# Attention scores in two passes over 128 stacked rows instead of three over 64

## The chip, the cores and the metric
One NeuronCore of a Trainium2 chip runs the whole program. The metric is device time in microseconds, the median over runs of one launch. The profile is one execution recorded by the hardware profiler.

## What is computed
A two-layer decoder trunk on 1024 tokens of width 1024, in float32. Layer 0 is a gated short convolution with a SwiGLU feed-forward block. Layer 1 is attention with 16 heads of width 64 over keys and values made once from the residual stream, again followed by a feed-forward block. Only the attention matters here:

```python
q = (x @ w_q).reshape(b, s, N_HEADS, HEAD_DIM) * (HEAD_DIM ** -0.5)
...
sc = jnp.einsum("bnqrhe,bnkrhe->bnrhqk", qb, k_cat).astype(jnp.float32)
...
sc = jnp.where(valid[:, None, None], sc + bias, -jnp.inf)
m = jnp.max(sc, axis=-1, keepdims=True)
p = jnp.exp(sc - m)
...
wts = jax.nn.softmax(jnp.stack(lses), axis=0)
o = jnp.sum(wts[..., None] * jnp.stack(outs), axis=0)
```

The three dilated branches are merged by their softmax denominators. The kernel computes this as one causal attention per head whose bias holds the ALiBi slope and the logarithm of how many branches see a key.

## The kernel before, in words
Float32 products are made from parts that TensorE takes in one pass (type fp32r): every operand is split into a high part and a low part, and a product is high·high + high·low + low·high, three passes that add up in PSUM. ScalarE makes high parts (a copy with a cast), VectorE low parts (a subtraction).

The program is written engine by engine. Each engine has its own list of instructions in a fixed order, and semaphores named after what is done (`q_lo_done`, `s_done`, `max_done`) tie them together. There is no scheduler: what stands in an engine's list behind a waiting instruction waits too. All weight loads stand in one list on SP (the SyncE queue).

The attention stage goes by pairs of heads, since two heads of 64 fill 128 partitions. There are 8 pairs. Six run in a loop of three turns with two pairs each, the last two are written out. A pair has 16 steps (`STEPS`): step `s` treats head `s // 8` of the pair and query block `s % 8` of 128 tokens, against the `s % 8 + 1` key blocks that it may see. A step with few blocks is short, one with eight is long. In step `s` TensorE does, in this order (`attend` in its block):

- `scores(s + 1)`: the scores of the next step, up to 1024 columns in the two SCORE banks, after VectorE has taken the maximum of the scores before (`max_done`),
- a third of the step's share of projection matmuls for the next pair,
- `turn_part(s - 2)`: one transpose of an output sum (`o_sum`),
- `turn_probs(s)`: the transposes of the exponentials, one per key block,
- a second third of the projection matmuls,
- `outputs(s - 1)`: probabilities times values, one matmul per key block,
- the last third.

Meanwhile VectorE adds the bias and takes the maximum (L1338), makes the low part of the transposed probabilities (L1354) and the output sum (L1370); ScalarE does the exponentials (L1005), the high part of the probabilities (L949), half of the output (L957) and the division (L965).

The projections of the next pair (keys, values, queries, each in two halves of 512 tokens, 24 matmuls per half) fill TensorE's time in between. They are cut into runs of three matmuls: 48 runs, and `slots` says how many runs each of the 16 steps gets. `END_RUNS` of the last step's runs are kept for the end of the pair, between the last outputs. `ends_in[j]` is the step in which half `j` ends (0, 1 keys, 2, 3 values, 4, 5 queries), and one step later ScalarE and VectorE turn it into high and low parts, behind their other work of that step. With `slots` all 3 this is step 14 for the first half of the queries. Its high and low parts are what the first score of the next pair, issued as `scores(16)` in step 15, needs:

```python
halves = moving * 2 + (2 * pair + 1 + i // 4)
pe.wait_ge(*q_lo_done.at("attn", halves))
...
passes = (("q_hi", "k_hi"), ("q_hi", "k_lo"), ("q_lo", "k_hi"))
```

A head's queries and keys lie in 64 of the 128 partitions (`rows`), so each score matmul contracts over 64 rows. Query parts have one buffer, key parts two (one per pair in turn).

Of the kernel before, what the change touches and what calls it, by code (L numbers as in the profile page):

```python
# [21 lines left out]
F32 = mybir.dt.float32  # L22
F32R = mybir.dt.float32r
# [3 lines left out]
ALU = mybir.AluOpType  # L27
ACT = mybir.ActivationFunctionType

P = 128  # L30
# [29 lines left out]
def trunk(nc, x, norm_g, conv_in_w, conv_w, conv_out_w, kv_norm_g, kv_w, q_w, o_w,  # L60
# [23 lines left out]
    with ExitStack() as ctx:  # L84
# [72 lines left out]
        spilled, x_back, stored = sem("spilled"), sem("x_back"), sem("stored")  # L157

# [125 lines left out]
        slots = [3, 3, 3, 3, 3, 3, 3, 3, 3, 3, 3, 3, 3, 3, 3, 3]  # L284
        END_RUNS = 3
# [8 lines left out]
        def _(sp):  # L294
            def column_chunk(w, col):

                return w.rearrange("(k p) n -> p k n", p=P)[:, :, bass.ds(col, P)]
# [12 lines left out]
            def load_two_row_blocks(ph, w):  # L310

                for c in range(KT):
                    half, q = c // (KT // 2), c % (KT // 2)
                    load((chunk0[ph] + c, 0),
                         w.rearrange("(k p) n -> p k n", p=P)[:, 2 * q:2 * q + 2,
                                                             half * HALF:(half + 1) * HALF])
# [50 lines left out]
            load_two_row_blocks("conv_out", conv_out_w[0])  # L367
            load_ffn("ffn0", 0)
            with sp.Fori(0, PAIRS // 2) as g:
                for pos in range(6):  # L370
                    col = g * (2 * P) + (pos // 3) * P
                    src = (kv_w, kv_w, q_w[0])[pos % 3]
                    load((chunk0["attn"] + pos, g * 6),
                         column_chunk(src, col + (D if pos % 3 == 1 else 0)))
            load_two_row_blocks("oproj", o_w[0])
# [8 lines left out]
        def _(pe):  # L384
# [214 lines left out]
            def attend(a, after):  # L599
# [6 lines left out]
                def scores(s):  # L606
                    pair, s_in = fixed + s // STEPS, s % STEPS
                    e, i = s_in // TT, s_in % TT
                    rows = slice(HD * e, HD * e + HD)
# [14 lines left out]
                    mm.then_inc(s_done.sem, 1)  # L624
# [87 lines left out]
            pe.wait_ge(*q_lo_done.at("attn", 1))  # L712
            for n, (q, k) in enumerate((("q_hi", "k_hi"), ("q_hi", "k_lo"), ("q_lo", "k_hi"))):
                mm = pe.matmul(psum[:, SCORE, 0:P], att[q][0:HD, 0:P], att[k][0:HD, 0, 0:P],
                               start=(n == 0), stop=(n == 2))
# [14 lines left out]
        def _(act):  # L730
# [178 lines left out]
            def project(r, j):  # L909

                moving, fixed = r
                part, h = j // 2, j % 2
                cols = slice(h * HALF, (h + 1) * HALF)
                product("attn", h, moving * 3 + (3 * fixed + part + 1),
                        moving * 3 + (3 * fixed + part + 1))
                if part == 0:
                    act.copy(att["k_hi"][:, fixed % 2, cols], bank(PROJ + h)) \
                        .then_inc(k_hi_done.sem, 1)
                elif part == 1:

                    act.wait_ge(*v_turned.at("attn", moving * 2 + (2 * fixed + h)))
                    act.copy(att["v_t"][:], bank(PROJ + h)).then_inc(v_done.sem, 1)
                else:

                    act.wait_ge(*s_done.at("attn", moving * STEPS
                                           + (fixed * STEPS - (1 - h) * TT // 2)))
                    act.activation(att["q_hi"][:, cols], bank(PROJ + h), ACT.Copy,
                                   scale=-float(HD) ** -0.5).then_inc(q_hi_done.sem, 1)
# [107 lines left out]
        def _(dve):  # L1036
# [254 lines left out]
            def project(r, j):  # L1291
# [5 lines left out]
                if part == 0:  # L1297
                    dve.wait_ge(*k_hi_done.at("attn", count))
                    dve.tensor_tensor(att["k_lo"][:, fixed % 2, cols], bank(PROJ + h),
                                      f32(att["k_hi"][:, fixed % 2, cols]), ALU.subtract) \  # L1300
                       .then_inc(k_lo_done.sem, 1)
                elif part == 2:
                    dve.wait_ge(*q_hi_done.at("attn", count))
                    dve.scalar_tensor_tensor(out=att["q_lo"][:, cols], in0=bank(PROJ + h),
                                             scalar=-float(HD) ** -0.5,
                                             in1=f32(att["q_hi"][:, cols]),
# [272 lines left out]
```

## Time and profile before

| | |
|---|---|
| median of 3 runs | 2700.91 us |
| lowest and highest | 2696.95 and 2702.74 us |
| span of the profiled execution | 2691.9 us |
| TensorE busy | 2549.6 us, 95% of the span |
| VectorE, ScalarE, GpSimd busy | 1120.2, 725.3 and 247.6 us |
| attention stage, pairs 1 to 7 and the last | from about 1225 to 1821 us of the span |

The span runs from the first to the last instruction; a run's time is some us longer, and for the profiled execution only the span is recorded. In the profile PE is TensorE, DVE is VectorE, ACT is ScalarE, POOL is GpSimd and SPq is the queue of SyncE. A line such as L620 is a line of the kernel before. Matmuls overlap in the pipeline and their ends are modelled, so what one costs is read from its start to the next start.

### The profile page before, as it was taken

Reading aid. Unit: us, or ns where it says so; the run is one execution under the profiler, and the core shown is the slowest. Engines: PE = TensorE matmul, PEld = TensorE weight load, DVE = VectorE, ACT = ScalarE, POOL = GpSimd, SP = SyncE. Lnnn points to the kernel's source line nnn. Section 1 sums busy time; section 2 is a strip of 40 time slices with the busy share of each in tenths; the row PEclk is TensorE's granted clock in tenths of the full one; section 3 lists DMA queues with packets and bytes.
Section 4 is the critical chain, followed back from the end, with each engine's and each line's share of the span. In section 5 each row is a group of like instructions: output and inputs, shape, how many; then the busy total and the mean of one; then the engine's idle time right before and its main releaser. Section 6 shows DMA issues by size and latency. Waiting matters only on the chain.

```text
span 2691.9 us, 32590 instructions
## 1 busy us (share of the span) xinstructions
PE 2549.6 (95%) x11648; PEld 2059.7 (77%) x11648; DVE 1120.2 (42%) x1686; ACT 725.3 (27%) x1328; POOL 247.6 (9%) x344
## 2 busy tenths in 40 slices
PE   7999989999999999969999999989799999999996
PEld 6888767888888888757777777767688888888885
DVE  4333243333333333574555555552533333333335
ACT  3111142111111111234544455552421111111112
POOL 1000031000000000241111111100500000000004
PEclk9999989999999999989999999989899999999998
DMA  4111111111111111120000000003021111111111
GB/s 126 47 54 47 55 40 48 47 50 51 47 47 47 47 47 48 38 83 28 24 20 20 24 16 24 24 1 118 24 63 47 47 47 47 47 47 47 47 47 70
DMA packets 162799, 124.18 MB, mean 46 GB/s; under 512 B 8736, under 2 KB 148000, under 8 KB 162720
## 3 DMA queue, kind: packets, MB, share of 16 engines
q1 hardware_dynamic: 159776, 111.71, 13.4%
q10 hardware_dynamic: 2944, 11.53, 1.2%
q8 instruction: 36, 0.59, 0.1%
q14 instruction: 43, 0.35, 0.0%
HBM read 114.84 MB, written 8.39 MB: 46 GB/s over the span
## 4 chain that ended last, share of the span: by engine, by line
PE 87%; issue 4%; POOL 3%; DVE 3%; ACT 2%; DMA 0%; SPq 0%; POOLq 0%; DVEq 0%; ACTq 0%
PE banks L397 46%; PE banks L539 17%; PE banks L583 9%; PE banks L474 5%; PE banks L620 5%; PE banks L632 2%; PE banks L645 2%; POOL resid L1483 2%; POOL rstd L1450 1%; PE banks L436 1%; PE banks L659 1%; POOL mean L1444 1%; DVE x_lo L1061 1%; ACT scores L1005 0%; ACT junk L773 0%
## 5 line engine op out<-in xcount | busy, mean ns | idle before, releaser
L1049 DVE TENSOR_TENSOR w_lo<-raw,w_hi 128x1024 fp32r<-128x1024 f32 x196 | 240.5, 1227 | 588.0 <-ACT w_hi L751 586.8
L397 PE MATMUL banks<-x_hi,w_hi 128*128 128x512 f32 x1792 | 449.1, 393 | 20.9 <-DVE x_lo L1061 20.9
L397 PE MATMUL banks<-x_lo,w_hi 128*128 128x512 f32 x1792 | 444.8, 390 | 0.0
L397 PE MATMUL banks<-x_hi,w_lo 128*128 128x512 f32 x1792 | 442.6, 389 | 0.0
L751 ACT CAST w_hi<-raw 128x1024 fp32r<-128x1024 f32 x196 | 205.5, 1049 | 809.6 <-PE banks L539 428.4
L397 PEld LDWEIGHTS banks<-x_hi,w_hi 128*128 128x128 f32 x1792 | 338.9, 190 | 93.8 <-issue 14.9
L397 PEld LDWEIGHTS banks<-x_lo,w_hi 128*128 128x128 f32 x1792 | 336.8, 188 | 69.8
L397 PEld LDWEIGHTS banks<-x_hi,w_lo 128*128 128x128 f32 x1792 | 336.4, 188 | 69.9
L1092 DVE TENSOR_TENSOR acc<-acc,banks 128x512 f32<-128x512 f32 x352 | 240.5, 687 | 209.4 <-PE banks L539 209.4
L539 PE MATMUL banks<-w_hi,hid_hi 128*128 128x512 f32 x704 | 224.4, 400 | 5.8 <-issue 4.7
L539 PE MATMUL banks<-w_lo,hid_hi 128*128 128x512 f32 x704 | 223.6, 399 | 0.0
L539 PE MATMUL banks<-w_hi,hid_lo 128*128 128x512 f32 x704 | 223.1, 398 | 0.0
L1214 DVE TENSOR_TENSOR hid<-silu_gate,banks 128x512 f32<-128x512 f32 x88 | 60.5, 688 | 319.9 <-PE banks L397 319.9
L539 PEld LDWEIGHTS banks<-w_hi,hid_hi 128*128 128x128 f32 x704 | 133.3, 190 | 38.7 <-issue 5.5
L539 PEld LDWEIGHTS banks<-w_lo,hid_hi 128*128 128x128 f32 x704 | 134.0, 190 | 32.5
L539 PEld LDWEIGHTS banks<-w_hi,hid_lo 128*128 128x128 f32 x704 | 133.7, 190 | 32.4
L870 ACT ACTIVATE silu_gate<-banks 128x512 f32<-128x512 f32 x88 | 52.8, 600 | 326.6 <-PE banks L397 326.5
L1354 DVE TENSOR_TENSOR pt<-banks,pt 128x128 fp32r<-128x128 f32 (+7 forms) x128 | 96.9, 757 | 100.3 <-ACT pt L949 100.2
L1338 DVE CUSTOM_DVE_ANT_0 scores<-banks,bias 128x128 f32<-128x128 f32 (+7 forms) x128 | 96.8, 756 | 95.1 <-PE banks L620 86.9
L583 PE MATMUL banks<-x_hi,w_hi 128*128 128x512 f32 x384 | 120.3, 426 | 11.2 <-DVE x_lo L1061 11.2
L583 PE MATMUL banks<-x_lo,w_hi 128*128 128x512 f32 x384 | 127.6, 423 | 0.0
L583 PE MATMUL banks<-x_hi,w_lo 128*128 128x512 f32 x384 | 117.0, 411 | 0.0
(116 smaller groups left out, 2631.1 us busy)
## 6 DMA issues: line engine op xcount, KB each, us to landing
raw<-in_ffn_in_w SPq DMA_DIRECT2D x88, 512.0 KB, 3.7
raw<-in_ffn_out_w SPq DMA_DIRECT2D x44, 512.0 KB, 3.2
raw<-in_conv_in_w SPq DMA_DIRECT2D x24, 512.0 KB, 3.7
raw<-in_kv_w SPq DMA_DIRECT2D x16, 512.0 KB, 3.9
resid<-in_x SPq DMA_DIRECT2D x8, 512.0 KB, 7.1
raw<-in_conv_out_w SPq DMA_DIRECT2D x8, 512.0 KB, 3.2
raw<-in_q_w SPq DMA_DIRECT2D x8, 512.0 KB, 3.8
x_spill<-resid ACTq DMA_DIRECT2D x1, 4096.0 KB, 12.8
```

Source lines behind the costliest of these rows:

```text
L397: mm = pe.matmul(bank(out_bank), w[:, slot, k * P:(k + 1) * P], a[:, k, h * HALF:(h + 1) * HALF], start=(i == 0), stop=(i == len(passes) - 1))
L474: mm = pe.matmul(bank(t), a[:, 2 * q + k, t * P:(t + 1) * P], w[:, slot, k * HALF:(k + 1) * HALF], start=(q == 0 and i == 0), stop=(last a ...
L539: mm = pe.matmul(bank(4 + o % 4), a[:, j, t * P:(t + 1) * P], w[:, a_slot(n + j), h * HALF:(h + 1) * HALF], start=(i == 0), stop=(i == len ...
L583: mm = pe.matmul(bank(PROJ + h), w[:, a_slot(chunk0["attn"] + c), k * P:(k + 1) * P], a[:, k, h * HALF:(h + 1) * HALF], start=(i == 0), st ...
L620: mm = pe.matmul(psum[:, SCORE + lo // HALF, 0:hi - lo], att[q][rows, i * P:(i + 1) * P], att[k][rows, pair % 2, lo:hi], start=(n == 0), s ...
L632: mm = pe.transpose(psum[:, PROB + j // 4, (j % 4) * P:(j % 4 + 1) * P], att["scores"][:, s % 2, j * P:(j + 1) * P], ident[:])
L751: act.copy(w_hi[:, n % SPLIT_RING, :], raw[:, s, :]).then_inc(hi_ready.sem, 1)
L1049: dve.tensor_tensor(w_lo[:, n % SPLIT_RING, :], raw[:, n % RAW_RING, :], f32(w_hi[:, n % SPLIT_RING, :]), ALU.subtract) \
L1092: dve.tensor_tensor(a, a, bank(4 + o % 4), ALU.add).then_inc(add_done.sem, 1)
L1214: dve.tensor_tensor(hid[:, h, :], silu_gate[:, h, :], bank(2 + h), ALU.mult).then_inc(hid_done.sem, 1)
L1338: dve.tensor_tensor_reduce(out=att["scores"][:, s % 2, 0:n], in0=two_banks(SCORE)[:, 0:n], in1=att["bias"][:, SEQ - n:SEQ], scale=1.0, sca ...
L1354: dve.tensor_tensor(att["pt"][:, s % 2, 1, 0:n], two_banks(PROB)[:, 0:n], f32(att["pt"][:, s % 2, 0, 0:n]), ALU.subtract) \
```

## The change
The score product is made in two passes over all 128 rows. For each head `e` a tile `q_stack[:, e]` holds the query's high part in partitions 0 to 63 and its low part in 64 to 127. A tile `k_stack[:, e, n]` holds the key's high part (`n` = 0) or low part (`n` = 1) in both halves of the partitions. Pass 0 then gives high·high + low·high, pass 1 high·low + low·low; the last product is new and was left out before.

The parts are first written side by side into `q_parts` (one half of 512 tokens at a time) and `k_parts`, each with one buffer. DMAs on SP copy them into the stacks: per pair 4 copies of 64 × 2048 values (512 KB) for the keys and 8 of 64 × 512 values (128 KB) for the queries. A copy waits until the parts are there (`k_lo_done`, `q_lo_done`) and until the scores that read the old stack are done (`s_done`). TensorE waits for the copies (`q_stacked`, `k_stacked`) and ScalarE waits for them before it writes the parts anew. The copies stand in SP's list between the weight loads. At the same time the table `slots` is changed, and `END_RUNS` goes from 3 to 2.

```diff
-                     ("q_hi", [SEQ], F32R), ("q_lo", [SEQ], F32R),
-                     ("k_hi", [2, SEQ], F32R), ("k_lo", [2, SEQ], F32R),
-
+                     ("q_parts", [2, HALF], F32R), ("k_parts", [2, SEQ], F32R),
+                     ("q_stack", [2, SEQ], F32R), ("k_stack", [2, 2, SEQ], F32R),
...
-        slots = [3, 3, 3, 3, 3, 3, 3, 3, 3, 3, 3, 3, 3, 3, 3, 3]
-        END_RUNS = 3
+        slots = [4, 4, 3, 3, 3, 2, 2, 2, 5, 4, 4, 3, 3, 2, 2, 2]
+        END_RUNS = 2
...
+            def stack_keys(r, e):
+
+                moving, fixed = r
+                sp.wait_ge(*k_lo_done.at("attn", moving * 2 + (2 * fixed + 2)))
...
+                sp.wait_ge(*s_done.at("attn", moving * STEPS + (fixed * STEPS - (1 - e) * TT)))
...
+                for b in range(2):
+                    sp.dma_start(att["k_stack"][b * HD:(b + 1) * HD, e].bitcast(F32),
+                                 att["k_parts"][e * HD:(e + 1) * HD].bitcast(F32)).then_inc(k_stacked[e], 16)
+
+            def stack_queries(r, h):
+
+                moving, fixed = r
+                cols = slice(h * HALF, (h + 1) * HALF)
+                for e in range(2):
+                    if e == 0:
+                        sp.wait_ge(*q_lo_done.at("attn", moving * 2 + (2 * fixed + h + 1)))
...
+                    sp.wait_ge(*s_done.at("attn", moving * STEPS
+                                          + (fixed * STEPS - (1 - e) * TT - (1 - h) * TT // 2)))
...
+                    for b in range(2):
+                        sp.dma_start(att["q_stack"][b * HD:(b + 1) * HD, e, cols].bitcast(F32),
+                                     att["q_parts"][e * HD:(e + 1) * HD, b].bitcast(F32)) \
+                            .then_inc(q_stacked[e], 16)
...
+            with sp.Fori(0, PAIRS // 2 - 1) as g:
+                for pp in range(2):
+                    load_projection(6 + 3 * pp, g)
+                    load_projection(7 + 3 * pp, g)
+                    stack_keys((g * 2, pp + 1), 0)
+                    load_projection(8 + 3 * pp, g)
+                    stack_queries((g * 2, pp + 1), 0)
+                    stack_keys((g * 2, pp + 1), 1)
+                    stack_queries((g * 2, pp + 1), 1)
...
-                    halves = moving * 2 + (2 * pair + 1 + i // 4)
-                    pe.wait_ge(*q_lo_done.at("attn", halves))
+                    if i % 4 == 0:
+                        halves = moving * 2 + (2 * pair + 1 + i // 4)
+                        pe.wait_ge(q_stacked[e], halves * 32)
+                    if i == 0:
+                        pe.wait_ge(k_stacked[e], moving * 32 + (pair + 1) * 32)
...
-                        passes = (("q_hi", "k_hi"), ("q_hi", "k_lo"), ("q_lo", "k_hi"))
-                        for n, (q, k) in enumerate(passes):
+                        for n in range(2):
                             mm = pe.matmul(psum[:, SCORE + lo // HALF, 0:hi - lo],
-                                           att[q][rows, i * P:(i + 1) * P],
-                                           att[k][rows, pair % 2, lo:hi],
-                                           start=(n == 0), stop=(n == 2))
+                                           att["q_stack"][:, e, i * P:(i + 1) * P],
+                                           att["k_stack"][:, e, n, lo:hi],
+                                           start=(n == 0), stop=(n == 1))
...
                 if part == 0:
-                    act.copy(att["k_hi"][:, fixed % 2, cols], bank(PROJ + h)) \
+                    for e in range(2):
+                        if fixed and h == 0:
+                            act.wait_ge(k_stacked[e], moving * 32 + fixed * 32)
+                    act.copy(att["k_parts"][:, 0, cols], bank(PROJ + h)) \
```

TensorE's list, step 13 of a pair, first before and then with the change. The first rows are the scores of step 14, L583 (then L650) the projections, L659 (L727) the output sum's transpose, L632 (L700) the transposed exponentials, L645 (L713) the outputs. Before:

```order
L620 MATMUL banks<-k_hi,q_hi 128x512
L620 MATMUL banks<-k_lo,q_hi 128x512
L620 MATMUL banks<-k_hi,q_lo 128x512
L620 MATMUL banks<-k_hi,q_hi 128x384
L620 MATMUL banks<-k_lo,q_hi 128x384
L620 MATMUL banks<-k_hi,q_lo 128x384
L583 MATMUL banks<-x_hi,w_lo 128x512 x3
L659 MATMUL banks<-ident,o_sum 128x128
L632 MATMUL banks<-ident,scores 128x128 x6
L583 MATMUL banks<-x_hi,w_hi 128x512 x3
L645 MATMUL banks<-pt,v_split 128x256 x5
L583 MATMUL banks<-x_hi,w_hi 128x512 x3
```

With the change:

```order
L688 MATMUL banks<-k_stack,q_stack 128x512 x2
L688 MATMUL banks<-k_stack,q_stack 128x384 x2
L650 MATMUL banks<-x_hi,w_hi 128x512 x2
L650 MATMUL banks<-x_lo,w_hi 128x512
L727 MATMUL banks<-ident,o_sum 128x128
L700 MATMUL banks<-ident,scores 128x128 x6
L650 MATMUL banks<-x_lo,w_hi 128x512 x3
L713 MATMUL banks<-pt,v_split 128x256 x5
```

Six score matmuls have become four, and of the three runs of projections the last, behind the outputs, is gone from this step. The projections are further on: they are in the second query half already.

TensorE's list at the end of a pair, from the outputs of step 14 to the last output sum. Before:

```order
L645 MATMUL banks<-pt,v_split 128x256 x7
L583 MATMUL banks<-x_lo,w_hi 128x512
L583 MATMUL banks<-x_hi,w_lo 128x512 x2
L659 MATMUL banks<-ident,o_sum 128x128
L583 MATMUL banks<-x_hi,w_lo 128x512 x3
L645 MATMUL banks<-pt,v_split 128x256 x8
L583 MATMUL banks<-x_hi,w_lo 128x512 x3
L659 MATMUL banks<-ident,o_sum 128x128
```

With the change:

```order
L713 MATMUL banks<-pt,v_split 128x256 x7
L650 MATMUL banks<-x_hi,w_lo 128x512 x3
L727 MATMUL banks<-ident,o_sum 128x128
L650 MATMUL banks<-x_hi,w_lo 128x512 x3
L713 MATMUL banks<-pt,v_split 128x256 x8
L727 MATMUL banks<-ident,o_sum 128x128
```

The run between the last outputs and the last transpose of the output sum is gone.

SP's list inside the loop, where before there were only the loads of the weights (`raw`), with the semaphore that each row waits for. With the change, from the load of the next query weights to the copies of the second query half:

```order
L308 DMA raw<-in_q_w 128x8x128 [waits lo_ready]
L395 REGISTER_ALU
L398 REGISTER_ALU [waits q_lo_done]
L403 DMA q_stack<-q_parts 64x512 [waits s_done]
L403 DMA q_stack<-q_parts 64x512
L398 REGISTER_ALU
L403 DMA q_stack<-q_parts 64x512 [waits s_done]
L403 DMA q_stack<-q_parts 64x512
L382 REGISTER_ALU [waits k_lo_done]
L386 DMA k_stack<-k_parts 64x2048 [waits s_done]
L386 DMA k_stack<-k_parts 64x2048
L403 DMA q_stack<-q_parts 64x512 [waits q_lo_done,s_done]
```

The first two copies of the query are those that the first score of the next pair waits for.

## Rows read from the trace of the kernel before
**Rows 1.** The page's chain of work that ended last, by engine

```profile
PE 87%; issue 4%; POOL 3%; DVE 3%; ACT 2%; DMA 0%; SPq 0%; POOLq 0%; DVEq 0%; ACTq 0%
```

**Rows 2.** Busy time in one pair: stretch, its length, engines (counts), clock, DMA

```profile
1245.92:1321.09 75.17, 72.33 (x385) 55.39 (x385) 39.65 (x93) 37.99 (x91) 10.95 (x19) 1.00 0.08 22
```

**Rows 3.** Timeline of TensorE's scores: start, duration, instruction, idle time before it

```profile
1321.02 0.49 PE L620 MATMUL banks<-k_hi,q_hi 64*128 64x512 f32 x1
1321.35 0.39 PE L620 MATMUL banks<-k_lo,q_hi 64*128 64x512 f32 x1
1321.58 0.39 PE L620 MATMUL banks<-k_hi,q_lo 64*128 64x512 f32 x1
1321.81 0.34 PE L620 MATMUL banks<-k_hi,q_hi 64*128 64x384 f32 x1
1321.99 0.34 PE L620 MATMUL banks<-k_lo,q_hi 64*128 64x384 f32 x1
...
1327.33 0.39 PE L620 MATMUL banks<-k_hi,q_lo 64*128 64x512 f32 x1
1327.65 0.74 PE L583 MATMUL banks<-x_hi,w_hi 128*128 128x512 f32 x2
...
1331.70 0.27 PE L620 MATMUL banks<-k_lo,q_hi 64*128 64x128 f32 x1
1331.81 0.27 PE L620 MATMUL banks<-k_hi,q_lo 64*128 64x128 f32 x1
...
1336.42 0.38 PE L620 MATMUL banks<-k_hi,q_hi 64*128 64x256 f32 x1 [0.24 <-DVE neg_max L1338]
1336.64 0.28 PE L620 MATMUL banks<-k_lo,q_hi 64*128 64x256 f32 x1
1336.76 0.28 PE L620 MATMUL banks<-k_hi,q_lo 64*128 64x256 f32 x1
```

**Rows 4.** Timeline of TensorE from step 13 to the next pair's step 1

```profile
1357.72 0.50 PE L620 MATMUL banks<-k_hi,q_hi 64*128 64x512 f32 x1
...
1362.78 0.50 PE L620 MATMUL banks<-k_hi,q_hi 64*128 64x512 f32 x1
...
1369.81 0.29 PE L620 MATMUL banks<-k_hi,q_hi 64*128 64x128 f32 x1 [1.51 <-DVE q_lo L1304]
...
1374.09 0.33 PE L659 MATMUL banks<-ident,o_sum 128*128 128x128 f32 x1 [1.09 <-DVE o_sum L1370]
...
1375.91 0.86 PE L583 MATMUL banks<-x_hi,w_lo 128*128 128x512 f32 x3
1376.75 0.33 PE L659 MATMUL banks<-ident,o_sum 128*128 128x128 f32 x1
...
1381.77 0.44 PE L620 MATMUL banks<-k_hi,q_hi 64*128 64x384 f32 x1 [1.44 <-DVE neg_max L1338]
```

**Rows 5.** Timeline of VectorE: the low part of the first query half

```profile
1368.97 0.69 DVE L1304 SCALAR_TENSOR_TENSOR q_lo<-banks,q_hi 128x512 fp32r<-128x512 f32 x1 [0.21 <-ACT q_hi L927]
```

**Rows 6.** DMA issues by line: count, KB each, median us from issue to landing

```profile
resid<-in_x SPq DMA_DIRECT2D x8, 512.0 KB, 7.1
...
result<-resid SPq DMA_DIRECT2D x8, 512.0 KB, 2.6
...
gains<-in_norm_g SPq DMA_DIRECT2D x1, 4.0 KB, 2.6
```

**Rows 7.** Timeline of SP's queue: one weight load's issue and the time it takes

```profile
1355.94 0.37 SPq L307 DMA_DIRECT2D raw<-in_kv_w  x1
```

**Rows 8.** The page's groups of instructions: count, busy us, mean ns, idle before

```profile
L1049 DVE TENSOR_TENSOR w_lo<-raw,w_hi 128x1024 fp32r<-128x1024 f32 x196 | 240.5, 1227 | 588.0 <-ACT w_hi L751 586.8
```

**Rows 9.** Busy time and clock at a pair's end and in the last pair

```profile
1368.30:1375.20 6.90, 4.29 (x30) 3.64 (x30) 4.00 (x9) 2.94 (x8) 0.52 (x2) 1.00 0.00 1
...
1755.00:1760.00 5.00, 3.47 (x18) 2.11 (x16) 2.16 (x9) 2.31 (x7) 0.32 (x1) 1.00 0.00 0
...
1761.70:1782.20 20.50, 20.50 (x74) 16.79 (x72) 8.81 (x22) 9.29 (x22) 1.61 (x5) 0.51 0.00 1
```

More of the change, by code:

```diff
@@ L157, in trunk @@
         spilled, x_back, stored = sem("spilled"), sem("x_back"), sem("stored")
+        k_stacked = [sem(f"k_stacked{e}") for e in range(2)]
+        q_stacked = [sem(f"q_stacked{e}") for e in range(2)]
         def signal(name, **per_phase):
@@ L308, in load, with load_row_block @@
                              if len(src.shape) == 3 else raw[:, s, :], src).then_inc(raw_in[s], 16)
[L310 to L316, printed above, removed]
+            def load_row_block(ph, w, c):
+                half, q = c // (KT // 2), c % (KT // 2)
+                load((chunk0[ph] + c, 0),
+                     w.rearrange("(k p) n -> p k n", p=P)[:, 2 * q:2 * q + 2,
+                                                         half * HALF:(half + 1) * HALF])
             def load_ffn(ph, layer):
@@ L366, in _ @@
                     load_conv_in(pos, g)
-            load_two_row_blocks("conv_out", conv_out_w[0])
+            for c in range(KT):
+                load_row_block("conv_out", conv_out_w[0], c)
             load_ffn("ffn0", 0)
[L369 to L374, printed above, removed]
@@ new lines, in _ @@
+            for pos in range(5):
+                load_projection(pos, 0)
+            stack_first()
+            with sp.Fori(0, PAIRS // 2 - 1) as g:
[7 more added lines that the diff above has]
+                    stack_queries((g * 2, pp + 1), 1)
@@ L376, in _ @@
+            load_row_block("oproj", o_w[0], 0)
+            stack_keys((0, PAIRS - 1), 0)
+            load_row_block("oproj", o_w[0], 1)
+            stack_queries((0, PAIRS - 1), 0)
+            stack_keys((0, PAIRS - 1), 1)
+            stack_queries((0, PAIRS - 1), 1)
+            for c in range(2, KT):
+                load_row_block("oproj", o_w[0], c)
             load_ffn("ffn1", 1)
@@ L711, in _ @@
                 project((0, 0), i)
[L712 to L715, printed above, removed]
+            pe.wait_ge(q_stacked[0], 32)
+            pe.wait_ge(k_stacked[0], 32)
+            for n in range(2):
+                mm = pe.matmul(psum[:, SCORE, 0:P], att["q_stack"][:, 0, 0:P],
+                               att["k_stack"][:, 0, n, 0:P], start=(n == 0), stop=(n == 1))
             mm.then_inc(s_done.sem, 1)
@@ L916, in project @@
                 if part == 0:
-                    act.copy(att["k_hi"][:, fixed % 2, cols], bank(PROJ + h)) \
+                    for e in range(2):
+                        if fixed and h == 0:
+                            act.wait_ge(k_stacked[e], moving * 32 + fixed * 32)
+                    act.copy(att["k_parts"][:, 0, cols], bank(PROJ + h)) \
                         .then_inc(k_hi_done.sem, 1)
@@ L923, in project @@
                 else:
-                    act.wait_ge(*s_done.at("attn", moving * STEPS
-                                           + (fixed * STEPS - (1 - h) * TT // 2)))
-                    act.activation(att["q_hi"][:, cols], bank(PROJ + h), ACT.Copy,
+                    for e in range(2):
+                        if fixed or h:
+                            act.wait_ge(q_stacked[e], moving * 64 + (2 * fixed + h) * 32)
+                    act.activation(att["q_parts"][:, 0], bank(PROJ + h), ACT.Copy,
                                    scale=-float(HD) ** -0.5).then_inc(q_hi_done.sem, 1)
@@ L1298, in project @@
                     dve.wait_ge(*k_hi_done.at("attn", count))
[L1299 to L1300 removed]
+                    dve.tensor_tensor(att["k_parts"][:, 1, cols], bank(PROJ + h),
+                                      f32(att["k_parts"][:, 0, cols]), ALU.subtract) \
                        .then_inc(k_lo_done.sem, 1)
```

36 lines of the change are left out of this document (31 added, 5 removed).

## The prediction, as made before the changed kernel ran
> **What bounds the kernel now.** I read three views. First the chain that ended last: 87% of it is TensorE work [rows 1], so what TensorE has to do sets the time almost everywhere. Second, the time by head pair inside the attention stage, the only stage that the change touches. One pair takes 75.2 us, TensorE is busy for 72.3 us of it at a full clock, VectorE for 39.7 and ScalarE for 38.0 [rows 2]. Seven pairs run so, three of them longer by a wait where the loop turns over (the last pair has no projections to fill with and is treated apart). Third, TensorE's instructions one by one, for the spacing of a pass and for the few waits.
>
> **The passes removed.** A pass costs its spacing from start to start, not the modelled duration. With 64 rows and 512 columns the spacing is 0.23 us, with 384 columns 0.18, with 256 columns 0.12, with 128 columns 0.11 [rows 3]. The projections contract over 128 rows with the same 512 columns, and three of them, started at 1375.91, have the next instruction ready to go 0.84 later [rows 4], about 0.23 each and the tail of the last, so a stacked pass should cost what a 64-row pass costs. A head has eight steps with 1 to 8 key blocks: 0.11 + 0.12 + 0.18 + 0.23 + 0.34 + 0.35 + 0.41 + 0.46 = 2.20 us for one pass. Two heads: **4.4 us per pair**.
>
> **The change of shape removed.** The first 64-row pass after a 128-row matmul takes 0.33 to the next start, not 0.23, and the first 128-row matmul behind the last 64-row pass comes 0.32 after it, not 0.23 [rows 3]. That is 0.1 us on the way in and 0.1 on the way out, at each of 16 score steps. All operands now have 128 rows, so I expect it to go: **3.2 us per pair**. The Trainium skill, "TensorEngine Tiling (Array Packing)", Key Properties, says that going from one tiling mode to another drains TensorE. By that rule the two gaps belong to the 64-row shape and go with it; without the rule they could be a cost of any change of instruction group, and the sum below would be 3.2 us per pair smaller.
>
> **The copies that the first score of a pair waits for.** Scores of the next pair begin in step 15 and need the first half of the query. Today VectorE's low part is made in step 14: that step starts on TensorE at 1362.78 (step 13 at 1357.72), the low part starts at 1368.97 and takes 0.69, so it ends 6.9 us into its step, and TensorE waits 1.51 for it [rows 4, 5]. The new table of slots brings it to step 13, where everything ahead of it is shorter: one pass (0.41), the two changes of shape (0.2), one block less in transposes, exponentials and outputs (about 0.3): 5.9 to 6.0 us into step 13. Step 13 becomes 5.06 − 0.41 − 0.2 − 0.69 (one run less; a run of three matmuls takes 3 × 0.23) = 3.8 us and step 14 becomes 5.52 − 0.46 − 0.2 − 0.69 = 4.2, so TensorE arrives at step 15 after 7.9 us. Between them lie two DMAs on SP's queue. The trace has no copy from SBUF to SBUF and nothing of 128 KB; its quickest transfers land after 2.6 us both at 4 KB and at 512 KB [rows 6], and one issue occupies the queue for 0.37 [rows 7]. So the second lands 3.0 after the low part, at 8.9: **a wait of 1.0 instead of 1.5, 0.5 us gained**. Bounds: no wait at all (1.5 gained), and a landing after 7.1 us, as for the x tiles that stood in a queue of eight [rows 6], which makes the wait 5.5 (4.0 lost). I take the low end, since at that moment SP's queue holds only these copies: the weight load issued ahead of them and the key copy of head 0 are due at steps 5 to 7.
>
> The page "DMA: Bandwidth & Descriptors" of the Trainium skill (section on the anatomy of one DMA) fits 2.0 us plus bytes over 436 GB/s for another issuing path. By it 128 KB would land after 2.3 and the wait would be 0.7 us, 2 us less over the kernel, an estimate from that page only; the 2.6 of the rows is what I use.
>
> The other copies: the keys are 2 MB per pair. Head 0's go out at step 6 or 7 and are needed at step 15, head 1's at step 14 and are needed in step 7 of the next pair, 30 us later. The second query half is ready at the end of the pair and needed three steps (11 us) later. They are hidden by that distance. Their traffic, 3 MB per pair, is 40 GB/s beside the 22 of today [rows 2], under which TensorE has next to no idle time; I cost it at nothing, with the late landing among the rivals if it isn't. SP also holds weight loads behind these copies, but a weight chunk is wanted a whole pair later.
>
> **What the new slots cost.** (a) Only two runs are kept for the end of a pair. Today one run stands between the last output matmuls and the last transpose: it starts at 1375.91 and the transpose at 1376.75 [rows 4], just when ScalarE's and VectorE's parts are done. Without it TensorE stands idle there: **0.75 lost** (the run itself moves elsewhere and costs the same). (b) In step 5 both a weight split (1.23 [rows 8]) and a key part (0.69, like the query's [rows 5]) now fall on VectorE while TensorE's step shrinks to 3.8. The next maximum comes late, and the score step behind it waits: **0.5 lost**, chosen between 0 and the split's whole 1.2. (c) The value projection of the first half now ends in step 9, and the query projection that reuses its bank starts at the top of step 10: **0.3 lost**. (d) The 0.24 us wait at step 8 [rows 3], late from today's split in step 6, goes: 0.25 gained. (e) Where the loop turns, TensorE waits 1.44 for a maximum in step 0 [rows 4]; the fourth run there covers 0.7 of it, three times in seven pairs: 0.3 gained per pair.
>
> **Sum.** Per pair 4.4 + 3.2 + 0.5 − 0.75 − 0.5 − 0.3 + 0.25 + 0.3 = 7.1; seven pairs 49.7. The last pair has no projections. 20.5 us of it run at about half the clock with TensorE never idle [rows 9]: a pass costs double there, so the four steps of 5 to 8 blocks save 2 × (0.34 + 0.35 + 0.41 + 0.46) = 3.1 us and some 0.4 for the shape; later steps partly wait for other engines, and I count 1.5 for them: 5. The first scores of all wait for a copy for perhaps 0.5. Total **54.2 us**. The profiled execution's span is 2691.9; the median 2700.91 stands 9.0 above it, and its own time outside the span is not recorded, so I take the 9.0 as unchanged: 2700.9 − 54.2 = **2646.7, say 2647 us**. Without a copy's wait, (b) and (c), it is 2.0 more per pair, 2633. Within 0.2% (5.4 us) is what a measurement of this kernel cannot tell from no change.
>
> **Rivals.**
> *The copies land late* (0.15). Landing after 7.1 costs 4.5 us more per pair, 31.5 in all: 2678. For it: four query copies and two of 512 KB are issued together. Against: the two that count are first in the queue.
> *The shape change stays, or other engines set the steps* (0.10). If 0.2 us per score step is not freed, seven pairs lose 22.4: 2669. If steps 5 to 7 and 13 to 14 are held by ScalarE's chain (part of the probabilities, then the exponentials), about as much. For it: the steps shrink to 3.8 and 4.2 us while ScalarE's and VectorE's work in them stays. Against: over the pair both are busy for little more than half of it [rows 2].
> *The clock falls at every pair's end* (0.10), the case that can end slower. Step 15 already holds waits of 1.51 and 1.09, and TensorE was busy for 4.29 of 6.90 us there without the clock falling; at the start of the last pair 3.47 of 5.00 was followed by clock 0.50 [rows 9]. With 1.0, 1.1 and 0.8 of waiting in step 15 it may fall in each pair. A spell costs half its length, since TensorE is busy throughout. Spells of 5 us would cost 17.5 over seven pairs: 2664. Spells of 20.5 us, as the one in the last pair [rows 9], cost 10.2 each, 72 in all: 2718, slower. It decides from 54.2 / 7 = 7.7 us per pair, spells of 15.5 us. The Trainium skill's "TensorE: Matmul & The Clock Gate" (Part 1) says the same in kind: idle time brings the half clock back. By that rule alone I could not tell how often.
> *Everything overlaps better* (0.05): 2633.
>
> **How the numbers follow.** The forecast has 0.60, with its own range 2633 to 2659. The late copy and the lost shape gain push up to 2680; below 2630 nothing but a mistake in the spacing leads. 2630 to 2680 leaves out the long clock spells (about 0.06) and some error. Faster 0.88; same 0.04; slower 0.08.
>
> **What would show it.** Score matmuls two per bank, 0.23 apart, and no 0.1 around them. A pair at 68 to 69 us where it was 75.2. TensorE's wait at the first score of a pair, on a DMA into the stacked query, near 1 us: above 3 the copy rival holds. A wait for the output sum of 0.7 to 0.9 at the pair's end. Clock 1.00 through the pairs, and the half-clock stretch of the last pair still there. Pairs with PE idle for more than 8 us, or a granted clock under 0.9 in them, would make the prediction wrong.

## The result and the profile after

| | before | with the change |
|---|---|---|
| median | 2698.93 us (4 runs, 2693.83 to 2702.74) | 2659.36 us (4 runs, 2658.29 to 2664.58) |
| ratio | | 0.9859, 95% interval 0.9843 to 0.9875 |
| span of the profiled execution | 2691.9 us | 2662.8 us |

The change makes the kernel faster by 39.6 us in the medians, 1.4% by the ratio; 54 us were forecast, and the time lies inside the range of 2630 to 2680. The two profiled executions differ by only 29.1 us. The changed kernel's own profiled run took 2664.58 us, 1.8 above its span, and it is the slowest of its four; by about the same distance the profiled run of before is its fastest (2693.83). What follows is read from the profiles, so it explains some 30 of the 40 us.

The chain that ended last, by engine, for the changed kernel (it answers to [rows 1]):

```profile
PE 84%; POOL 4%; DVE 4%; ACT 3%; issue 3%; DMA 1%; SPq 0%; POOLq 0%; DVEq 0%; ACTq 0%
```

TensorE and "issue" have lost four points to GpSimd, VectorE, ScalarE and a DMA, one to each. Two pairs of the attention stage and the whole stage, busy time and clock as in [rows 2], first the changed kernel:

```profile
1291.69:1364.42 72.73, 64.44 (x361) 54.04 (x361) 40.22 (x93) 38.48 (x91) 11.51 (x19) 0.98 0.29 67
1364.42:1438.44 74.02, 65.10 (x360) 54.18 (x361) 38.41 (x93) 38.66 (x91) 11.55 (x19) 0.98 0.28 64
...
1222.90:1793.60 570.70, 495.07 (x2778) 414.54 (x2777) 313.53 (x733) 306.60 (x724) 84.47 (x148) 0.97 0.26 61
```

and the kernel before, the like pair and the whole stage:

```profile
1294.62:1369.81 75.19, 72.35 (x384) 55.39 (x385) 39.66 (x93) 38.00 (x91) 10.94 (x19) 1.00 0.08 22
1221.87:1822.30 600.43, 561.88 (x2970) 432.21 (x2969) 316.05 (x733) 303.58 (x724) 80.19 (x148) 0.98 0.07 19
```

The stage is 29.7 us shorter, so nothing else moved. This pair takes 72.73 us where it took 75.19: 2.5 gained, not 7.1. By the first scores of each pair, the seven pairs gained 22.7 us together, 3.2 each, and the last pair 7.0 (66.1 us where it took 73.2). In the pair shown TensorE's busy time fell by 7.9, more than the 7.6 that were forecast for passes and shape. What is left came back as idle time: 72.73 − 64.44 = 8.3 us instead of 2.8.

All waits of TensorE in that pair, from its timeline (the wait stands in brackets at the end):

```profile
1295.75 0.33 PE L727 MATMUL banks<-ident,o_sum 128*128 128x128 f32 x1 [1.09 <-DVE o_sum L1443]
1298.41 0.33 PE L727 MATMUL banks<-ident,o_sum 128*128 128x128 f32 x1 [0.68 <-DVE o_sum L1443]
...
1325.00 0.44 PE L688 MATMUL banks<-k_stack,q_stack 128*128 128x128 f32 x2 [1.14 <-DVE neg_max L1411]
1326.75 0.33 PE L727 MATMUL banks<-ident,o_sum 128*128 128x128 f32 x1 [0.56 <-DVE o_sum L1443]
...
1338.87 1.63 PE L650 MATMUL banks<-x_hi,w_hi 128*128 128x512 f32 x6 [0.47 <-ACT v_t L994]
...
1346.53 0.45 PE L727 MATMUL banks<-ident,o_sum 128*128 128x128 f32 x1 [2.15 <-DVE v_split L1387]
...
1364.42 0.44 PE L688 MATMUL banks<-k_stack,q_stack 128*128 128x128 f32 x2 [2.19 <-DMA q_stack<-q_parts]
```

They add up to 8.3. The last is the wait for the copies; it is 1.25 to 1.30 in most pairs and 2.19 in this one. The 1.14 and 0.56 are step 7, the 0.47 is the value bank at the top of step 10. The largest that the prediction didn't have at all is the 2.15 in step 11: the transpose of the output sum shares a PSUM bank with the transposed values and must wait until their low part is taken. This is that place in an earlier pair, on the other engines:

```profile
1271.03 1.90 POOL L1581 TENSOR_TENSOR raw<-raw,gains 128x1024 f32<-128x1024 f32 x1
...
1273.03 1.05 ACT L820 CAST w_hi<-raw 128x1024 fp32r<-128x1024 f32 x1 [0.61 <-POOL raw L1581]
1273.98 0.58 ACT L994 COPY v_t<-banks 128x512 f32<-128x512 f32 x1
1274.11 1.23 DVE L1122 TENSOR_TENSOR w_lo<-raw,w_hi 128x1024 fp32r<-128x1024 f32 x1 [1.37 <-ACT w_hi L820]
1274.46 0.59 ACT L1006 CAST v_split<-banks 128x512 fp32r<-128x512 f32 x1
1275.26 0.68 DVE L1387 TENSOR_TENSOR v_split<-banks,v_split 128x512 fp32r<-128x512 f32 x1
```

GpSimd scales a weight chunk (1.90). ScalarE stands at the head of its list waiting for it, and behind it stand the copy of the second value half and the high part of the first. VectorE's split and the value's low part follow. None of these engines is busy for much over half of a pair, but the table has put this work into one step: with all slots 3 the value halves end in steps 7 and 10, with the new table in 8 and 9.

The granted clock falls there too. The stretch that begins during that wait, in the pair whose waits are listed above, and below it two rows of TensorE's timeline in it:

```profile
1345.51:1348.93 3.42, 2.40 (x9) 2.13 (x10) 2.06 (x5) 1.44 (x3) 0.32 (x1) 0.60 0.00 0
```

```profile
1346.77 1.06 PE L700 MATMUL banks<-ident,scores 128*128 128x128 f32 x4
1347.48 0.78 PE L650 MATMUL banks<-x_lo,w_hi 128*128 128x512 f32 x1
```

The mean granted clock is 0.60 of full speed here, mostly its lower level of 1.2 GHz. Four transposes take 0.71 us to the next start; at full clock they take 0.36 (1310.15 to 1310.51 in the same pair). Behind the first microseconds of the stage, the seven pairs of before were at full clock throughout. In the changed kernel six of seven have one such stretch of some 3.5 us, but not all at this place: three come with the 2.15 wait (near 1346, 1421 and 1493), three in step 7 with two waits of together 1.5 to 1.7 (near 1547, 1619 and 1691), and with four waits of 1.98 to 2.15 in step 11 none came.

### The profile page after: what moved, and what is told of

It is laid out like the page before. It is cut to its first block, busy times and chain, and to the rows that moved or that the text cites. A ratio compares the mean times of both kernels' runs of the same rounds, so it can differ in the third digit from the quotient of the medians.

```text
span 2662.8 us, 32310 instructions
## 1 busy us (share of the span) xinstructions
PE 2483.0 (93%) x11456; PEld 2043.2 (77%) x11456; DVE 1117.8 (42%) x1686; ACT 728.0 (27%) x1328; POOL 251.6 (9%) x344
## 4 chain that ended last, share of the span: by engine, by line
PE 84%; POOL 4%; DVE 4%; ACT 3%; issue 3%; DMA 1%; SPq 0%; POOLq 0%; DVEq 0%; ACTq 0%
PE banks L464 46%; PE banks L606 17%; PE banks L650 8%; PE banks L541 6%; PE banks L700 2%; PE banks L688 2%; POOL resid L1556 2%; PE banks L713 1%; POOL raw L1581 1%; POOL rstd L1523 1%; PE banks L503 1%; PE banks L727 1%; POOL mean L1517 1%; DMA q_stack<-q_parts 1%; ACT w_hi L820 1%
## 5 line engine op out<-in xcount | busy, mean ns | idle before, releaser
L464 PE MATMUL banks<-x_hi,w_hi 128*128 128x512 f32 x1792 | 449.2, 393 | 21.7 <-DVE x_lo L1134 21.7
L464 PE MATMUL banks<-x_lo,w_hi 128*128 128x512 f32 x1792 | 445.6, 390 | 0.0
L464 PE MATMUL banks<-x_hi,w_lo 128*128 128x512 f32 x1792 | 442.6, 389 | 0.0
L650 PE MATMUL banks<-x_hi,w_hi 128*128 128x512 f32 x384 | 114.0, 416 | 14.4 <-DVE x_lo L1134 11.2
L650 PE MATMUL banks<-x_lo,w_hi 128*128 128x512 f32 x384 | 120.4, 415 | 0.0
L688 PE MATMUL banks<-k_stack,q_stack 128*128 128x256 f32 (+1 forms) x382 | 95.0, 357 | 25.9 <-DVE neg_max L1411 15.9
L1581 POOL TENSOR_TENSOR raw<-raw,gains 128x1024 f32<-128x1024 f32 x26 | 49.9, 1921 | 718.0 <-DMA raw<-in_kv_w 703.7
```

Source lines behind the costliest of these rows:

```text
L464: mm = pe.matmul(bank(out_bank), w[:, slot, k * P:(k + 1) * P], a[:, k, h * HALF:(h + 1) * HALF], start=(i == 0), stop=(i == len(passes) - 1))
L650: mm = pe.matmul(bank(PROJ + h), w[:, a_slot(chunk0["attn"] + c), k * P:(k + 1) * P], a[:, k, h * HALF:(h + 1) * HALF], start=(i == 0), st ...
L688: mm = pe.matmul(psum[:, SCORE + lo // HALF, 0:hi - lo], att["q_stack"][:, e, i * P:(i + 1) * P], att["k_stack"][:, e, n, lo:hi], start=(n ...
L1581: pool.tensor_tensor(w, w, gain.unsqueeze(2).broadcast_to([P, KT, P]), ALU.mult) \
```

## The experiments

My theory after the profile: stacking itself gives what was forecast or more, and the new table of slots takes most of it back, by a jam of the weight chunk and the value parts on ScalarE and VectorE. The rival: the copies cost it, by their wait or their traffic. Each ratio below is to the kernel before, from runs on the same chip.

**e1: the table alone.** The kernel before, with only

```diff
-        slots = [3, 3, 3, 3, 3, 3, 3, 3, 3, 3, 3, 3, 3, 3, 3, 3]
-        END_RUNS = 3
+        slots = [4, 4, 3, 3, 3, 2, 2, 2, 5, 4, 4, 3, 3, 2, 2, 2]
+        END_RUNS = 2
```

> The kernel before with the new table of slots and END_RUNS = 2, and nothing else: three passes over 64 rows, no copies. My theory: the new table brings a jam of its own (in steps 9 to 11 the scaling of a weight chunk on GpSimd, its split and the value parts fall together, and the end of the pair loses its cover), and only the copies need it. It should remove the 1.5 us wait for the query at a pair's start, and bring about 0.7 at the pair's end and 1 to 2 us of waiting for the value's low part: between 5 us faster and 10 us slower than the kernel before. The rival, that the table is harmless and the copies cost the time: 8 to 12 us faster than before, TensorE idle for about 1.5 us per pair, not 2.8.

Measured 2710.52 us, ratio 1.0057 (1.0035 to 1.0080): 11 us slower, just beyond my range, and the rival's sign is wrong. Without a single copy waits of the same kinds appear, here on TensorE's timeline of e1, ahead of them one whole pair:

```profile
1296.45:1373.65 77.20, 72.58 (x386) 56.36 (x385) 39.36 (x93) 38.41 (x92) 10.90 (x19) 1.00 0.07 21
```

```profile
1279.80 0.30 PE L659 MATMUL banks<-ident,o_sum 128*128 128x128 f32 x1 [1.45 <-DVE v_split L1314]
1297.74 0.33 PE L659 MATMUL banks<-ident,o_sum 128*128 128x128 f32 x1 [0.75 <-DVE o_sum L1370]
1301.56 0.33 PE L659 MATMUL banks<-ident,o_sum 128*128 128x128 f32 x1 [1.09 <-DVE o_sum L1370]
1304.21 0.33 PE L659 MATMUL banks<-ident,o_sum 128*128 128x128 f32 x1 [0.68 <-DVE o_sum L1370]
```

The wait for the query is gone, as it should be. The jam at the values (1.45), a late output sum in step 15 (0.75) and the bare end itself (0.68) have taken its place, and the pair is 2.0 us longer than before (77.20 against 75.19). In step 7 e1 waits only 0.29 for the maximum and 0.32 for the output sum, so the 1.14 and 0.56 of the changed kernel need the shorter steps of the stacked scores too.

**e2: the copies with the old table.** The changed kernel with the lines of e1's diff turned back.

> The changed kernel with the old table (all slots 3, END_RUNS = 3). My theory: the waits for the value's low part (2.15 us), for the value bank (0.47) and at the pair's end (0.68) go, TensorE's wait at the first score of a pair grows from 1.3 to 5 or 6 us, since the low part is made one step later and the copies of 3 us come on top; in sum about the time of the changed kernel, 2655 to 2670, with the granted clock the open point. The rival, that the copies cost the time: the wait at the first score is 5 to 6 all the same, but the other waits stay too, and it is over 2680.

Measured 2658.23 us, ratio 0.9856 (0.9840 to 0.9873): the same as the changed kernel. The wait for the copies is now the large one, and the one for the values is small (TensorE's timeline of e2):

```profile
1278.05 0.30 PE L727 MATMUL banks<-ident,o_sum 128*128 128x128 f32 x1 [0.58 <-DVE v_split L1387]
1290.18 0.44 PE L688 MATMUL banks<-k_stack,q_stack 128*128 128x128 f32 x2 [4.58 <-DMA q_stack<-q_parts]
```

So the new table buys 3.3 us of the copies' wait per pair and pays as much elsewhere: turning it back gains nothing. The loss belongs to the two together; the copies need an earlier query, and this table is a dear way to get it. In e2 the clock falls at the 4.3 to 4.6 us wait of every pair.

**e3: two passes over 64 rows.** The kernel before without the product of the query's low and the key's high part:

```diff
-                        passes = (("q_hi", "k_hi"), ("q_hi", "k_lo"), ("q_lo", "k_hi"))
+                        passes = (("q_hi", "k_hi"), ("q_hi", "k_lo"))
```

> The kernel before without the third pass (query low part times key high part is left out of the scores): two passes over 64 rows, old table, no copies. It separates the pass from the change of shape. By my theory TensorE's busy time per pair falls from 72.4 by 4.4 to 68.0 us, and the first and last score matmul of a group keep their 0.1 us; the changed kernel has 64.4, so 3.2 to 3.5 us per pair are the shape's. The rival, that the 0.1 us are no matter of the 64 rows: busy 64.5 to 65. Time by my theory 2667 to 2675.

Measured 2665.52 us, ratio 0.9880 (0.9864 to 0.9897), 1.5 us beyond my range. One pair of e3, and below it one of e8, a run with stacked operands whose pairs keep a full clock:

```profile
1293.27:1364.22 70.95, 67.98 (x360) 51.52 (x361) 39.53 (x93) 37.91 (x91) 11.11 (x19) 1.00 0.08 23
```

```profile
1286.26:1352.52 66.26, 62.85 (x361) 52.61 (x361) 39.61 (x93) 38.42 (x91) 11.35 (x19) 1.00 0.33 74
```

The pass is worth 72.35 − 67.98 = 4.4 us per pair, as forecast. Between e3 and e8 the busy time falls by 67.98 − 62.85 = 5.1, not 3.2. Beside the shape they differ in the table and the scaling, which by e9 are worth 0.2 of it (a pair of e9 is busy for 72.15, of before for 72.35), so 4.9 are the shape's. My expectation compared with the changed kernel's 64.44, which holds some 1.6 us of half clock. The missing part stands in the matmuls beside the scores. TensorE's timeline at the like place of both kernels shows a run of three projection matmuls, the scores behind it and, for the changed kernel, the run that follows. The kernel before:

```profile
1330.74 0.86 PE L583 MATMUL banks<-x_lo,w_hi 128*128 128x512 f32 x3
1331.53 0.32 PE L620 MATMUL banks<-k_hi,q_hi 64*128 64x128 f32 x1
```

and the changed kernel:

```profile
1282.08 0.86 PE L650 MATMUL banks<-x_hi,w_hi 128*128 128x512 f32 x3
1282.78 0.98 PE L688 MATMUL banks<-k_stack,q_stack 128*128 128x512 f32 x4
1283.60 0.63 PE L650 MATMUL banks<-x_hi,w_hi 128*128 128x512 f32 x2
```

A run of three ahead of the scores takes 0.79 to the next start before and 0.70 after: a third tenth of a microsecond that I had put down to the run. The four stacked score matmuls take 0.82 with the change into and out of them, which is the plain 2 × 0.23 + 2 × 0.18. So going to 64 rows and back costs about 0.3 us per group of scores (4.9 / 16). That a change of tiling mode drains TensorE is what the Trainium skill says ("TensorEngine Tiling (Array Packing)", Key Properties); the two runs agree in that the cost goes with the shape, but the drain itself is seen in none.

**e4: the scaling one step earlier.** The changed kernel with

```diff
-                        for c, step in enumerate((0, ends_in[1], ends_in[3])):
+                        for c, step in enumerate((0, ends_in[1] - 1, ends_in[3] - 1)):
```

in GpSimd's list.

> The changed kernel with the second and third scaling of a weight chunk on GpSimd one step earlier (steps 3 and 8 instead of 4 and 9). My theory: ScalarE's high part of the chunk then doesn't wait for GpSimd, everything behind it in steps 5 and 10 comes some 0.6 to 1 us earlier, the wait for the value's low part falls from 2.15 to about 1.3 and the one for the maximum in step 7 from 1.2 to 0.5, and the clock's short spells at step 11 may end: 2645 to 2654. The rival, that the copies' traffic or their wait set the time: 2657 to 2661, unchanged.

Measured 2647.32 us, ratio 0.9812 (0.9796 to 0.9829): 12 us better than the changed kernel from GpSimd's order alone. ScalarE's high part no longer waits, and TensorE's wait falls (timeline of e4):

```profile
1271.38 1.05 ACT L820 CAST w_hi<-raw 128x1024 fp32r<-128x1024 f32 x1
1272.33 0.58 ACT L994 COPY v_t<-banks 128x512 f32<-128x512 f32 x1
...
1345.70 0.30 PE L727 MATMUL banks<-ident,o_sum 128*128 128x128 f32 x1 [1.44 <-DVE v_split L1387]
```

The waits alone are about 1 us per pair, 7 in all. The rest fits the clock: its low level comes once in the seven pairs of e4, at a wait of 1.87 for the copies, and no longer in steps 7 and 11, where it came six times. The wait for the maximum in step 7 fell from 1.14 to 0.86 only, less than expected.

**e5: high copies first.** The changed kernel, where SP issues the copies of the query's high part for both heads after `q_hi_done` and those of the low part after `q_lo_done`:

```diff
-                for e in range(2):
-                    if e == 0:
-                        sp.wait_ge(*q_lo_done.at("attn", moving * 2 + (2 * fixed + h + 1)))
+                for b, done in enumerate((q_hi_done, q_lo_done)):
+                    sp.wait_ge(*done.at("attn", moving * 2 + (2 * fixed + h + 1)))
...
+                    for e in range(2):
```

> The changed kernel with the query copies in another order: the two copies of the high part are issued when ScalarE has made it, the two of the low part when VectorE has, so that one copy, not two, stands between the low part and the first score. One issue of such a copy occupies SP's queue for 0.6 us. My theory, that the copies sit on the path only at this one place: the wait at the first score falls from 1.27 to 0.7 in each pair, 4 us in all, 2653 to 2657. The rival, that the copies' traffic costs time elsewhere too: unchanged order of waits and less than 2 us.

Measured 2660.71 us, ratio 0.9862 (0.9846 to 0.9879): no gain, where 2653 to 2657 was expected. TensorE still waits for the copies at the first score of a pair, 1.15 to 1.22 us in five pairs and 1.77 in one. The four issues on SP's queue, started as soon as the high part was there:

```profile
1287.81 2.39 SPq L403 DMA_DIRECT2D q_stack<-q_parts  x4
```

Four take 2.39, 0.6 each. The low copy of head 0 comes third and is issued some 1.2 us after the first, 0.7 us after its part is ready; in the changed kernel it was 0.8. My edit had only swapped which copies stand ahead of it.

**e6: a table that keeps the end and moves the values apart.** The changed kernel with

```diff
-        slots = [4, 4, 3, 3, 3, 2, 2, 2, 5, 4, 4, 3, 3, 2, 2, 2]
-        END_RUNS = 2
+        slots = [4, 4, 3, 3, 3, 2, 2, 2, 4, 4, 4, 3, 3, 2, 2, 3]
+        END_RUNS = 3
```

> The changed kernel with another table: 4, 4, 3, 3, 3, 2, 2, 2, 4, 4, 4, 3, 3, 2, 2, 3 and END_RUNS = 3, so one run moves from step 8 to the end of the pair, and the second value half ends one step later than before (step 10), the query as in the changed kernel (step 12). My theory: the 0.68 at the pair's end goes, and so does the jam of step 10, since the value halves are two steps apart (wait for the low part under 1 us, none for the value bank), while the value's second low part now stands ahead of the query's in step 13 and adds about 0.7 to the wait for the copy: 2 us per pair and the short clock spells with it, 2640 to 2650. The rival, that the waits follow the amount of work and not the place of the value halves: 2655 to 2660.

Measured 2637.62 us, ratio 0.9778 (0.9762 to 0.9794), better than expected. One run moved from step 8 to the pair's end gives 22 us; it also makes the second value half and its weight chunk one step later. The 0.68 and the 0.47 are gone, the value's wait is 0.56, and the wait for the copies did not grow by the 0.7 that I had charged. A pair of e6 at full clock:

```profile
1289.66:1357.40 67.74, 63.02 (x360) 52.56 (x361) 38.98 (x93) 38.28 (x91) 11.71 (x19) 1.00 0.31 71
```

**e7: e4, e5 and e6 together.**

> The table of the run before, the high copy first, and the scaling one step earlier, together. If the three causes are separate, their gains add: 4 us from the copy, some 12 from the scaling with the clock and 5 to 10 more from the table: 2632 to 2642. If they are one and the same jam seen at three places, it is no better than the early scaling alone, 2645 to 2648.

Measured 2627.77 us, ratio 0.9740 (0.9723 to 0.9756). On top of the table the early scaling gives another 10 us, if the order of the copies gives as little as it did in e5. So these two are separate causes: alone e4, e5 and e6 changed the time by −12, +1 and −22 us, together by −32. My sum was too small because e6 gave more than I had put in.

**e8: the same with the query parts free of the values.** As e7, with another table:

```diff
-        slots = [4, 4, 3, 3, 3, 2, 2, 2, 4, 4, 4, 3, 3, 2, 2, 3]
+        slots = [4, 4, 3, 3, 3, 3, 2, 2, 3, 5, 3, 3, 2, 2, 3, 3]
         END_RUNS = 3
```

> As the run before with the table 4, 4, 3, 3, 3, 3, 2, 2, 3, 5, 3, 3, 2, 2, 3, 3 and END_RUNS = 3: value halves end in steps 7 and 9, the query's first half in step 12 as in the changed kernel, so nothing stands ahead of the query's parts in step 13. My theory: no jam at the values, no added wait for the copy, all covers in place: TensorE idle for 3 to 4 us per pair, 2630 to 2638. The rival, that the step in which a weight chunk and a value half fall together is what counts (step 10 here as in the changed kernel): wait for the value's low part stays over 1 us and 2645 or more.

Measured 2621.29 us, ratio 0.9715 (0.9693 to 0.9737), 9 us better than my range. TensorE's idle time in the pair shown under e3 is 66.26 − 62.85 = 3.4 us. The waits for the values were gone in e7 already; what e8 adds is another thing. The wait for the maximum in step 7 falls from 0.85 (at 1321.14 in e7) to 0.16 (at 1319.30 in e8), and up to that step the two tables differ only in a third run in step 5. The copies' wait falls to about 0.5 in four of six pairs.

**e9: that table for the 64-row scores.** The kernel before with e8's table and e4's scaling.

> The kernel before (three passes over 64 rows, no copies) with the table and the earlier scaling of the run e8. It tells how much of e8's gain is the stacking's and how much a better table's. My theory, that the waits of the kernel before are 2.8 us per pair and mostly at the pair's start: the earlier query takes the 1.5 away and little else, 2688 to 2696, so that stacking is worth 65 to 75 us once the table fits. The rival, that e8's table is better for any scores: 2670 or less.

Measured 2686.29 us, ratio 0.9961 (0.9944 to 0.9977; the runs spread from 2672 to 2692), 2 us beyond my range. The better table is worth 10 us without stacking, so most of e8's gain is not the table's own.

**e10: the copies of head 0 first.** As e8, with the order high 0, low 0, high 1, low 1, each issued when its part is there.

> The run e8 with the four query copies in the order high and low part of head 0, then of head 1, where the high one doesn't wait for the low part. In e5 the two high copies of both heads filled SP's queue, 0.6 us each, and the low one came third. My theory: now the low part of head 0 is issued at once when it is ready, the wait at the first score falls from 1.14 to about 0.5, 4 us over the kernel: 2616 to 2619. The rival, that the time from issue to landing is set by something else than the queue: unchanged at 2621.

Measured 2616.49 us, ratio 0.9705 (0.9689 to 0.9721), the lowest median here, though its interval overlaps that of e8. The trace is clearer than the times: TensorE doesn't wait for the copies in any pair. In the one that begins at 1285.90 it is busy for 63.12 of 65.60 us.

```profile
1285.90:1351.50 65.60, 63.12 (x363) 52.87 (x363) 39.85 (x94) 38.41 (x91) 11.42 (x19) 1.00 0.33 76
```

## Why the prediction was right and where it was off

The time lies in the range, and that is partly luck. The 9.0 us between the span and the median, which the prediction kept unchanged, were mostly the spread of the runs: the profiled run of before lasted 2693.83, 7 below the 2700.91 that the prediction started from. From profile to profile 29.1 us were gained where 54.2 were forecast. By two of its own signs the prediction fails: TensorE is idle for 8.3, 8.9 and 8.7 us in three of the six pairs from 1291.69 on (6.8 to 7.4 in the others), and over 8 was to make it wrong; and a pair takes 71.5 to 74.0 us, not 68 to 69. A small slip besides: the copy's wait, (b) and (c) sum to 1.8 and not 2.0.

- *The pass*: 4.4 us per pair forecast, 4.4 measured (e3). Right.
- *The change of shape*: 3.2 forecast, about 5 measured (e3 against e8). The mechanism was right and the term too small: I read the gap on both sides of the scores and missed the one inside the run ahead of them.
- *The copies' wait*: 1.0 forecast, 1.25 to 1.30 in most pairs. A 128 KB copy lands 2.3 us after its issue, not 2.6, but its issue takes 0.6, not 0.37; the two errors nearly cancel, which is luck, and e10 shows that the queue was the part one could remove. The fit of the Trainium skill that the prediction cites gives 2.3 us for the transfer, which the row matches; the wait of 0.7 that followed from it does not.
- *The traffic*: nothing forecast. The durations of the other engines' work didn't change (GpSimd's scaling took 1.90 before and after), and e1 shows the jam at the values without any copy. Right as far as the runs show.
- *(a) the bare end of the pair*: 0.75 forecast, 0.68 measured. *(d)*: the wait is gone. Right.
- *(b) split and key part in step 5*: 0.5 forecast, 1.14 + 0.56 = 1.7 measured in step 7, beyond the 1.2 that I gave as its bound. I had followed the maximum and not the output sum behind it on VectorE, and I had left out that the split waits for GpSimd. That wait is the smaller part: the early scaling took 0.28 off the 1.14 (e4), a third run in step 5 another 0.7 (e8 against e7). So it is mostly the rival that I gave 0.10, other engines setting short steps. The split and the key part stood together in the kernel before too (VectorE at 1332.72 and 1333.87), with a wait of 0.24 behind them. The 0.56 stays in e8 and e10.
- *(c) values in step 9*: 0.3 forecast for the bank (0.47 measured), and the step that failed most: I followed the second half's bank and not the first half's parts, which stand behind the weight chunk. It is the 2.15 us of step 11. Together (b) and (c) cost 4.3 us per pair where 0.8 was forecast.
- *(e) the wait where the loop turns over*: 0.3 per pair forecast; the waits are 1.38 and 1.15 where they were 1.44 and 1.43, under 0.1 per pair.
- *The last pair*: 4.5 us forecast, 7.0 measured. Its stretch of half clock, which was expected to stay, lasted 20.5 us before and now comes as one of 8 us and one of 4.
- *The clock*, a rival at 0.10, came true in its mild form, though inside the pairs and not at their ends: one short stretch at the low level in six of seven, 1.6 us of TensorE's time each (64.44 against the 62.85 of e8). They go when the waits do (one left in e4 and one in e6, none in e8).

For the pair above: 9.5 of TensorE's work gained (72.35 − 62.85), 1.6 lost to the clock, 5.4 lost to waits: 2.5. The gain of 39.6 in the medians holds some 10 us more than the profiles show, 5 on either side: the profiled run was the fastest of the kernel before and the slowest of the changed one. Which part of the kernel varies was not looked at. In the pair that waits 2.19 for its copies and not 1.27, the second copy landed 3.3 us after its issue and not 2.3; why is open.

## What to carry to other kernels

When operands are arranged so that a matmul fills all rows, count the gaps around the group and not the passes alone: here the gaps were worth more than the pass. When a table that places work is changed to make one thing earlier, walk every engine's list through the steps that it touches, GpSimd's too: a wait of 0.61 us at the head of ScalarE's list, which is half idle, was worth most of 12 us over the kernel, with the clock stretches that went with it (e4). Where the change makes TensorE's steps shorter, leave it work in the steps in which another engine's list is long (e8). And test the table without the change and the change without the table: e1 showed that the table costs time by itself, e2 that turning it back only moves the loss to the copies, and e6 to e10 that a better table keeps the gain of stacking.

## What the runs showed of the hardware that was not expected

- The issue of one copy between SBUF tiles from SP's queue takes 0.6 us (2.39 for four), a weight load's 0.37 [rows 7]. Copies of 512 KB, 64 × 8 KB, issued in twos, land 6.3 us after their issue, 128 KB after 2.3 (medians); from the DMA view of the changed kernel:

```profile
k_stack<-k_parts SPq DMA_DIRECT2D x32, 512.0 KB, 6.3
...
q_stack<-q_parts SPq DMA_DIRECT2D x64, 128.0 KB, 2.3
```

- A group of 64-row matmuls between 128-row ones costs about 0.3 us beyond its passes (e3 against e8, less the 0.2 us per pair of e9).
- TensorE's clock stood at the low level for some 3.5 us in six pairs of the changed kernel whose waits there were far shorter: three times with one of 2.15 us, three times with two of 1.5 to 1.7 together. One wait's length does not decide it: at the same place the low level came with three of seven waits in e1 (1.3 to 1.5) and with none of seven in e4 (1.4).
